# A hybrid decoder step on one core: new order of the recurrent block's activations, of the first norm's loads and of the sample rows

## What is computed

```
xn = rmsnorm(x, norm_mix)
lru_x, lru_g, q, k, v = split(xn @ w_in)
xc = causal_conv(x_ext, w_conv, b_conv)
r = sigmoid(block_diag(w_a) xc + b_a);  i = sigmoid(block_diag(w_x) xc + b_x)
log_a = -8 * r * softplus(-lam);  a = exp(log_a)
u = sqrt(-expm1(2 * log_a)) * i * xc        # factor 1 at position 0
h_t = a_t * h_(t-1) + u_t
y_lru = (h * gelu(lru_g)) @ w_branch_lru
```

## Time and profile before

| | |
|---|---|
| median of 3 runs | 1946.58 us (1945.2 to 1947.05) |
| the profiled execution | 1945.86 us, of which the span from first to last instruction is 1944.1 us |
| PE busy | 1918.2 us, 99% of the span |
| DVE, ACT, POOL busy | 1145.4, 616.8, 873.3 us |
| mean granted TensorE clock | 0.998 of full speed |
| chain that ended last | PE 88%, DVE 5% |

### The profile page before, as it was taken

One profiled execution on the slowest core, in us unless ns is written; L12 is line 12 of the kernel. 1 busy time (PEld: TensorE's weight loads), 2 busy tenths in 40 slices (PEclk: granted clock), 3 DMA queues, 4 the chain that ended last, 5 costly groups with the idle time before them and its releaser, 6 DMA issues.

```text
span 1944.1 us, 34565 instructions
## 1 busy us (share of the span) xinstructions
PE 1918.2 (99%) x13148; PEld 1870.2 (96%) x13148; DVE 1145.4 (59%) x1373; ACT 616.8 (32%) x1035; POOL 873.3 (45%) x533
## 2 busy tenths in 40 slices
PE   7999999999999999999999999999999999999999
PEld 7899999999999999999999999999999999999999
DVE  5666688878844545444328663586554555455555
ACT  5655632222203333333320111333222232223222
POOL 3233254444434433534334332336655656455643
PEclk9999999999999999999999999999999999999999
DMA  6111112222254355544345652112111111211112
GB/s 244 43 46 35 45 70 86 86 86 86 87 171 131 128 158 173 171 160 149 128 161 182 209 194 87 65 33 66 50 39 50 61 55 34 65 45 61 34 59 110
DMA packets 85034, 191.73 MB, mean 99 GB/s; under 512 B 10445, under 2 KB 38600, under 8 KB 83408
## 3 DMA queue, kind: packets, MB, share of 16 engines
q1 hardware_dynamic: 57872, 142.92, 22.3%
q10 hardware_dynamic: 27072, 47.53, 7.1%
HBM read 147.81 MB, written 42.62 MB: 98 GB/s over the span
## 4 chain that ended last, share of the span: by engine, by line
PE 88%; DVE 5%; issue 2%; DMA 1%; ACT 1%; POOL 1%; ACTq 1%; SPq 0%; DVEq 0%; POOLq 0%
PE ups L726 30%; PE ups L870 14%; PE ups L995 13%; PE ups L1038 11%; PE aux L1038 8%; PE aux L910 3%; PE ups L889 2%; PE aux L900 1%; PE ups L767 1%; PE aux L809 1%; DVE x L1583 1%; DMA big_f<-x_R 1%; PE aux L754 1%; PE ups L900 1%; ACTq L1090 1%
## 5 line engine op out<-in xcount | busy, mean ns | idle before, releaser
L726 PE MATMUL ups<-big,wsp 128*128 128x344 f32 x4680 | 755.1, 321 | 0.7 <-issue 0.7
L726 PEld LDWEIGHTS ups<-big,wsp 128*128 128x128 f32 x4680 | 739.9, 188 | 8.8 <-issue 1.6
L564 POOL CAST wsp<-wraw 128x1024 fp32r<-128x1024 f32 (+1 forms) x96 | 104.6, 1089 | 658.0 <-issue 393.9
L674 POOL TENSOR_TENSOR wsp<-wraw,wsp 128x512 fp32r<-128x512 f32 x184 | 263.7, 1449 | 212.4 <-ACT wsp L1406 212.4
L870 PE MATMUL ups<-big,wsp 128*128 128x344 f32 x1728 | 302.6, 326 | 0.0
L870 PEld LDWEIGHTS ups<-big,wsp 128*128 128x128 f32 x1728 | 271.4, 189 | 3.5 <-issue 3.0
L995 PE MATMUL ups<-big,wsp 128*128 128x344 f32 x1584 | 254.4, 320 | 0.3 <-DVEq L1979 0.2
L995 PEld LDWEIGHTS ups<-big,wsp 128*128 128x128 f32 x1584 | 248.9, 188 | 3.9 <-issue 2.9
L1038 PE MATMUL ups<-big,wsp 128*128 128x258 f32 x1920 | 240.7, 283 | 1.4 <-ACT ext L1445 1.3
L1038 PEld LDWEIGHTS ups<-big,wsp 128*128 128x128 f32 x1920 | 234.9, 189 | 1.8 <-issue 1.8
L566 POOL TENSOR_TENSOR wsp<-wraw,wsp 128x1024 fp32r<-128x1024 f32 (+1 forms) x96 | 228.7, 2382 | 7.7
(11 more groups left out here) (248 smaller groups left out, 1870.5 us busy)
## 6 DMA issues: line engine op xcount, KB each, us to landing
wraw<-w_in SPq DMA_DIRECT2D x52, 512.0 KB, 3.9
wraw<-w_ffn_in SPq DMA_DIRECT2D x80, 256.0 KB, 2.6
x<-out_qkv SPq DMA_DIRECT2D x35, 512.0 KB, 4.2
out_qkv<-x ACTq DMA_DIRECT2D x32, 512.0 KB, 3.3
wraw<-w_ffn_out SPq DMA_DIRECT2D x44, 256.0 KB, 2.8
x<-gate_s SPq DMA_DIRECT2D x16, 516.0 KB, 4.6
wraw<-w_merge SPq DMA_DIRECT2D x16, 512.0 KB, 6.7
x<-o_s SPq DMA_DIRECT2D x8, 792.0 KB, 4.8
```

The lines of the kernel that those rows point to most:

```text
L564: nc.gpsimd.tensor_copy(hi, raw).then_inc(w_hi, 1)
L674: nc.gpsimd.tensor_tensor(lo, raw_at(b), hi.bitcast(F32), ALU.subtract).then_inc(f_lo, 1)
L726: ins = nc.tensor.matmul(ups[:, slot, c, 0:CH], wsp[:, slot, w, k, :], src[:, a, k, c * CH:(c + 1) * CH], start=(k == 0 and n == 0), stop= ...
```

## The change

Four things are moved. In ACT's loop, gate chunk 0 of the next tile comes ahead of gelu and root, both of which now stand at the end of the iteration, and gates 1 and 2 follow each other; tanh is written to U instead of onto R. At the start, all x tiles are loaded ahead of weight tile (0,1), the rows of x ahead of weight tile (1,0); the lambda operations come first; DVE makes the low half of weight tile (0,0) and POOL's second split waits for six low halves of x; DVE squares row block 7, and a dummy root loads the table before block 6. The gate weights and the bias lines are issued by SP instead of ACT. The sample rows' work comes ahead of the last V tile, with its root one V tile earlier.

```diff
--- before.py
+++ after.py
@@ sync (SP's queue)
+            def gate_weights(i):
+                sp.wait_ge(gate_mm, i * NCH + 1)
+                for a, wn in enumerate(("w_rg_a", "w_rg_x")):
+                    src = A[wn][0].rearrange("n i j -> (n i) j")
+                    for h in range(2):
+                        sp.dma_start(bd[h * HD:(h + 1) * HD, a, h * HD:(h + 1) * HD],
+                                     src[ds(i * P + h * HD, HD), :]).then_inc(bd_loaded, 16)
-            sp.dma_start(gmix[:], A["c_norm_mix"]).then_inc(gm_ld, 16)
+            for dst, con in ((gmix[:], A["c_norm_mix"]), (par[:], A["c_par"])):
+                sp.dma_start(dst, con).then_inc(gm_ld, 16)
...
                 if name == "lru":
                     first = 2
                     weights(0, 0)
-                    x_tiles(0, 3)
+                    x_tiles(0, KT)
                     weights(0, 1)
-                    x_tiles(3, KT)
-                    for dst, con in ((par[:], A["c_par"]), (ident[:], A["c_ident"]), (x_rows[8], A["x_R"][SEQ:NT])):
+                    for dst, con in ((ident[:], A["c_ident"]), (x_rows[8], A["x_R"][SEQ:NT])):
                         sp.dma_start(dst, con).then_inc(par_ld, 16)
-                    weights(1, 0)
                     for n in range(4):
                         sp.dma_start(big2_f32[:, 0, 2 * n:2 * n + 2, 0:D],
                                      A["x_R"][2 * n * P:2 * (n + 1) * P].rearrange("(b p) d -> p b d", p=P)).then_inc(row_loaded[n], 16)
-                    weights(1, 1)
+                    weights(1, 0)
                     for dst, con in consts:
                         sp.dma_start(dst, con).then_inc(const_ld, 16)
+                    sp.wait_ge(bd_zero, 1)
+                    gate_weights(0)
...
+                    weights(1, 1)
...
+                if name == "qk":
+                    first = 1
+                    weights(0, 0)
+                    gate_weights(KT - 1)
+                    weights(0, 1)
                 with sp.Fori(first, iters) as i:
                     for slot in range(2):
                         weights(i, slot)
+                        if name == "lru" and slot == 0:
+                            gate_weights(i - 1)
@@ gpsimd
                 if name == "lru":
                     first = 1
-                    split(name, nk, 0, 0)
+                    pool.wait_ge(w_loaded[0], 16)
+                    nc.gpsimd.tensor_copy(wsp[:, 0, 0], wraw[:, 0]).then_inc(w_hi, 1)
+                    pool.wait_ge(xl_done, 6)
                     split(name, nk, 0, 1)
@@ scalar
...
+            act.wait_ge(gm_ld, 32)
             act.wait_ge(lam_dve, 1)
             nc.scalar.activation(lamt[:, 1, :], lamt[:, 0, :], ACT.Exp, scale=-1.0).then_inc(lam_act, 1)
             act.wait_ge(lam_dve, 2)
             nc.scalar.activation(lamt[:, 3, :], lamt[:, 2, :], ACT.Ln).then_inc(lam_act, 1)
...
             for k in range(KT):
                 high(k)
-            for b in range(SEQ // P + 1):
+            for b in (8, 0, 1, 2, 3, 4, 5):
                 square(b)
+            nc.scalar.activation(st[:, 0:1], epst[:], ACT.Sqrt)
+            square(6)
...
-            def side(i):
-                gate(i, 1)
+            def gelu(i):
                 act.wait_ge(ge_raw, i + 1)
                 nc.scalar.activation(GE, GE, ACT.Gelu_apprx_tanh)
-                gate(i, 2)
 
             def decay(i):
                 act.wait_ge(gate_ev, i * NCH + (NCH + 1))
                 apart(act)
-                step.step(nc.scalar.activation(AD, R, ACT.Exp, scale=cdec[:, 0, ds(i, 1)]))
-                apart(act)
-                nc.scalar.activation(R, R, ACT.Tanh, scale=cdec[:, 1, ds(i, 1)]).then_inc(ath_done, 1)
+                nc.scalar.activation(AD, R, ACT.Exp, scale=cdec[:, 0, ds(i, 1)])
+                nc.scalar.activation(U, R, ACT.Tanh, scale=cdec[:, 1, ds(i, 1)]).then_inc(ath_done, 1)
+                act.wait_ge(ath_done, i + 1)
+
+            def root_of(i):
                 act.wait_ge(m2_done, i + 1)
                 nc.scalar.activation(M2, M2, ACT.Sqrt).then_inc(sqrt_done, 1)
 
             with act.Fori(1, KT) as i:
-                step.loop(i, 1, 1)
-                side(i - 1)
-                gate_weights(i)
+                gate(i - 1, 1)
+                gate(i - 1, 2)
                 front(i)
                 decay(i - 1)
                 gate(i, 0)
-            step.end(KT - 1)
+                gelu(i - 1)
+                root_of(i - 1)
...
-            side(KT - 1)
...
+            gate(KT - 1, 1)
+            gelu(KT - 1)
+            gate(KT - 1, 2)
+            decay(KT - 1)
             first_evac()
-            act.wait_ge(m2_done, KT)
-            nc.scalar.activation(M2, M2, ACT.Sqrt).then_inc(sqrt_done, 1)
+            root_of(KT - 1)
...
                 if n == 2:
                     act.wait_ge(row_mm, 1)
                     nc.scalar.activation(QKR.rearrange("p a h e -> p (a h e)"), aux[0:RW, 1, 0:2 * P], ACT.Copy).then_inc(row_act, 1)
-                if n == 3:
                     act.wait_ge(row_dve, ROW_SQUARED)
@@ vector
-            for k in range(KT):
-                low(k)
-            dve.wait_ge(par_ld, 48)
-
+            dve.wait_ge(gm_ld, 32)
...
+            dve.wait_ge(w_hi, 1)
+            nc.vector.tensor_tensor(wsp[:, 0, 1], wraw[:, 0], wsp[:, 0, 0].bitcast(F32), ALU.subtract).then_inc(w_split[0], 1)
+            for k in range(KT):
+                low(k)
...
+            dve.wait_ge(row_loaded[3], 16)
+            step.step(nc.vector.tensor_tensor(x_rows[7], x_rows[7], x_rows[7], ALU.mult))
+            nc.vector.tensor_reduce(row_rms[:, 7:8], x_rows[7], AX_X, ALU.add).then_inc(nsq_done, 1)
             dve.wait_ge(nsq_done, SEQ // P + 2)
             nc.vector.reciprocal(row_rms, row_rms).then_inc(rr_done, 1)
...
-                nc.vector.scalar_tensor_tensor(M2, M2, 1.0, R, ALU.add, ALU.mult).then_inc(m2_done, 1)
+                nc.vector.scalar_tensor_tensor(M2, M2, 1.0, U, ALU.add, ALU.mult).then_inc(m2_done, 1)
...
-            v_in(3)
-            dve.wait_ge(ps_free[1], T0["att0"] + 1)
-            dve.wait_ge(u_sb, 2)
-            dve.sem_inc(pt_ev, 2)
...
+            dve.wait_ge(u_stored, 16)
+            dve.wait_ge(v_stored[1], 16)
+            dve.wait_ge(qn_stored[0], 16 * 13)
+            nc.vector.memset(VTOK[:, :, :, HD:HD + 1], 1.0)
+            v_in(3)
+            dve.wait_ge(ps_free[1], T0["att0"] + 1)
+            dve.wait_ge(u_sb, 2)
+            dve.sem_inc(pt_ev, 2)
+            for s, n in ((sa_done, 2), (pt_mm, 2), (pv_mm, 2), (o_ev, 1)):
+                dve.sem_inc(s, n)
```

More of the change, by code:

```diff
@@ L449, in _ @@
                                      A["x_R"][2 * n * P:2 * (n + 1) * P].rearrange("(b p) d -> p b d", p=P)).then_inc(row_loaded[n], 16)
-                    weights(1, 1)
+                    weights(1, 0)
                     for dst, con in consts:
                         sp.dma_start(dst, con).then_inc(const_ld, 16)
+                    sp.wait_ge(bd_zero, 1)
+                    gate_weights(0)
+                    sp.dma_start(lines.rearrange("p (g n) -> p g n", g=NG), A["c_lines"].rearrange("g b n -> b g n")).then_inc(lines_ld, 16)
+                    sp.dma_start(relx[0:NBK, :], A["rel_bias"]).then_inc(lines_ld, 16)
+                    sp.dma_start(relx[NBK:NBK + 1, :], A["c_one"]).then_inc(lines_ld, 16)
+                    weights(1, 1)
                 if name == "merge":
@@ L738, in norm_rows @@
                 pe.wait_ge(rr_done, 1)
-                pe.wait_ge(par_ld, 48)
+                pe.wait_ge(par_ld, 32)
                 for b in range(SEQ // P):
@@ L1084, in _ @@
             step = Chain(act, s_act)
[L1085 to L1091, removed]
             act.wait_ge(ones_done, 1)
             nc.scalar.activation(st[:, 0:1], epst[:], ACT.Copy)
-            act.wait_ge(gm_ld, 16)
+            act.wait_ge(gm_ld, 32)
+            act.wait_ge(lam_dve, 1)
+            nc.scalar.activation(lamt[:, 1, :], lamt[:, 0, :], ACT.Exp, scale=-1.0).then_inc(lam_act, 1)
+            act.wait_ge(lam_dve, 2)
+            nc.scalar.activation(lamt[:, 3, :], lamt[:, 2, :], ACT.Ln).then_inc(lam_act, 1)
             def high(k):
@@ L1105, in square @@
                 else:
-                    act.wait_ge(par_ld, 48)
+                    act.wait_ge(par_ld, 32)
                 n = x_rows[b].shape[0]
@@ L1189, in first_evac @@
                 nc.scalar.activation(sqkv[:, 0, :], tmp(0)[:, SEQ:NT], ACT.Copy).then_inc(sqc_done, 1)
-            side(KT - 1)
-            act.wait_ge(gate_ev, KT * NCH + 1)
-            step.step(nc.scalar.activation(AD, R, ACT.Exp, scale=cdec[:, 0, KT - 1:KT]))
-            nc.scalar.activation(R, R, ACT.Tanh, scale=cdec[:, 1, KT - 1:KT]).then_inc(ath_done, 1)
+            gate(KT - 1, 1)
+            gelu(KT - 1)
+            gate(KT - 1, 2)
+            decay(KT - 1)
             first_evac()
-            act.wait_ge(m2_done, KT)
```

(16 more changed lines are left out.)

## The result

The changed kernel takes 1952.49 us (median of 8 runs, 1951.06 to 1953.9), the kernel before beside it 1946.8 (8 runs, 1945.13 to 1947.3): 1.0032 times as long, 95% interval 1.0021 to 1.0043. The profiled spans are 1949.9 and 1944.1 us. The forecast was 1951.9.

A forecast was written before the change was run, and what follows sets the result against it. TensorE (PE) was taken as the bound, busy 1918.2 of 1944.1 us. Gains of 9.6 against losses of 14.9 gave +5.3 on the 1946.58 median: 1951.9 us, range 1944.0 to 1957.0 (the forecast case's own 1948.5 to 1955).

The forecast's parts named there:

- the gate waits: Recurrent loop: PE's waits of 1.33 and 1.15 us for gate(i,0)'s sigmoids vanish as the gate goes first, 2.5 us gained.
- slot at g + 16.25: Loop: PSUM slot 1 freed 16.25 us after PE's gates(i,0) start (g), needed at g + 14.6; 1.7 us wait each iteration.
- gate path: Loop: gate(i,1) stands behind the root, so PE's third gates wait 1.15 us, counted as lying inside the 1.7.
- Rival 1: Loop's slack holds, so only the gains stay: 1937.0 us, chance 0.12.
- rival 2: Start gives less, rows no earlier and clock still falls: gain 1.5 instead of 5.0, 1955.4 us, chance 0.14.
- rival 3: Loop: only the 1.15 of the gate path is paid because DVE's tail runs ahead: 1947.9 us, chance 0.05.
- rival 4: ACT's table switches each cost a drain as long as the load, 26.9 us more: 1978.8 us, chance 0.01.
- The hand-over: From recurrent loop to QK: the last root ends late, so PE waits 2.1 us for the statistics, 1.8 more than before.
- the loop's head: First iteration: a table load stands in front of a gate PE already awaits, 0.8 us lost (bounds 0 and 1.2).
- The norm: Start: x's rows land sooner and the row norm comes at 32.7, gain 3.4 us (bounds 2.2 and 4.9).
- The clock after the norm: Start: a stand cut to 1.5 us no longer drops PE's clock to half, 1.6 us saved (bounds 0 and 1.6).
- The sample rows: Before the first scores: the row work moves into DVE's idle time ahead of the last V tile, 2.1 us gained.

The follow-up runs named there:

- a_old_order: Changed kernel with ACT's loop back in the old order (gelu, then root ahead of gate 0), all else as changed: 1939.98 us, ratio 0.9965.
- b_loop_alone: Kernel before with only ACT's new loop order and tanh to U, gate weights still issued by ACT: 1959.31 us, ratio 1.0066.
- r2_root_ahead: Changed kernel with root ahead of gelu behind gate 0, run once more for its trace: 1946.92 us.
- q_peeled: Changed kernel with gelu ahead of gate 0, first and last turn written out of the loop, last turn's root ahead of its gate 0: 1936.28 us, ratio 0.9948.
- w_warm: Changed kernel with 24 dummy 128 x 128 matmuls on PE ahead of the first tile: 1953.23 us, ratio 1.0037.
- v_gelu_ahead: Changed kernel with gelu moved ahead of gate 0 in ACT's loop, root still behind that gate: 1939.57 us, ratio 0.9961.
- s_start_alone: Changed kernel with ACT's old loop order and the sample rows back behind the last V tile: 1945.4 us, ratio 0.9991.
- r_root_ahead: Changed kernel with root ahead of gelu behind gate 0, the product waiting for gelu: 1945.93 us, ratio 0.9993.

## Why the prediction was right, point by point

**Right in its sum and in the loop.** For the order in ACT's queue the prediction had 14.9 us of losses and 2.5 of gain at the gate waits, 12.4 net. Between the two traces, from gates(0,0) to the second statistics, it is 12.0 (230.0 after, 218.1 before); the medians of a_old_order and b_loop_alone give 12.5 and 12.4, with what the clock takes behind the stands in them. The turn was put at 27.8 us and is 27.87; root at g + 8.5 (g + 8.53), slot at g + 16.25 (g + 16.25), gate path 1.15 (1.13). The terms were durations in series on ACT and then on DVE, each with an uncontended row, and that is why they held. Two smaller sizes were off and offset each other only in part. The first turn costs less, 27.32 (66.29 to 93.61), as PE waits for the slot six times and not seven. The two gate waits bring more than their 2.5: the turns with them take 27.74 and 27.55 instead of 26.13, 3.0 together. Rival 1 (the slack holds) needed this chain to be shorter; rival 2 (a norm after 34 with a fallen clock) didn't happen, the norm is at 33.18; rival 3 is what r2_root_ahead does, which takes gelu out of the root's path; rival 4 (a drain at each table switch) has no time to stand in, as the loads and activations of the rows above follow one another without a gap.

**The hand-over** was put at 2.1 us of wait and is 2.41; **the loop's head** at 0.8 and is 0.64. q_peeled takes both away.

**The norm**: 2.9 instead of 3.4. The last chunk of rows came at 30.03 rather than 29.5. A wrong step stood beside it: "PE done with tile 7 some 2 us earlier", from which followed that PE was ready at 31.2. PE was ready at 32.87. The change feeds x faster, but some thirty matmuls at the start are slow whatever feeds them (w_warm). The upper bound of 4.9 for this gain was therefore out of reach. More than that, "worth nothing while the rows arrive last" holds only in some executions. With the same loads, the last chunk was there at 28.9 to 29.2 us in v_gelu_ahead, q_peeled, r2_root_ahead and s_start_alone, and PE came to the norm without a wait at 32.42 to 32.89 (also in a_old_order, at 33.12):

```profile
32.42 1.95 PE L763 MATMUL aux<-ident,big_f 128*128 128x128 f32 x16
```

There PE's own work is what the norm waits for, and earlier rows would bring nothing.

**The clock after the norm**: 1.6 predicted. From row norm to gates(0,0) it is 13.96 us before (36.09 to 50.05) and 12.73 after (33.18 to 45.91), so 1.2. And it is no fixed property of the kernel before: b_loop_alone has the same start, stood for 2.77 us at the same place, and the clock (the column behind PE's) stayed:

```profile
36.13 2.05 PE L741 MATMUL aux<-ident,big_f 128*128 128x128 f32 x16 [2.77 <-DVE big_f L1544]
...
37.00:38.00 1.00, 1.00 (x11) 1.00 0.00 0
```

Its 16 matmuls take 2.05 us, where the earlier trace rows has 3.17. This term should have had a chance beside its price.

**The sample rows** are the term that was mis-sized: 2.1 predicted, 3.7 between the two traces. The wait was counted and the clock behind it was not, though the prediction had done so for the norm. (1.33 leaves the clock alone, 2.94 doesn't) gave no side for 2.11; the windows behind the wait would have. But the 1.6 is not a certain part either: in b_loop_alone PE stood 2.10 us at the same place and the clock stayed at 1.00. By the same rule the hand-over's new wait of 2.41 has a price beyond its length in some executions: behind 2.40 in b_loop_alone the clock fell, behind 2.41 in the changed kernel's profiled execution it did not. The prediction left this out too, with the opposite sign.

**What made up for it.** The running difference was +4.1 at 592.86 us, 1.1 under the forecast's, and +5.8 at the end. The 1.7 between them lie in the feed-forward loop, which the change doesn't touch (the chain that ended last, start and length):

```profile
1417.27 17.22 PE ups L995 x108
...
1606.57 17.22 PE ups L995 x108
```

```profile
1421.38 17.22 PE ups L1017 x108
...
1611.55 17.22 PE ups L1017 x108
```

Three turns take 189.30 us before and 190.17 after, 63.10 or 63.39 each. Over nine turns the kernel before took 569.6 us, the changed one 571.3, and the experiments from 570.0 to 572.3. What makes a turn 0.28 longer wasn't found; no idle time of PE is shown there. So the profiled total agrees with the forecast better than its terms do, and that part is luck. Against the forecast the start gave 0.9 us less and the turns 2 to 7 cost 0.9 less, the hand-over cost 0.4 more; the sample rows gave 1.6 more, and the feed-forward loop, which is in no term, took 1.7.

## What to carry to other kernels

When an instruction that waits for the bound engine moves ahead in a queue, add up everything that is queued behind it up to what frees that engine's next buffer; the slack has to hold all of it. A cheap order puts ahead of the waiting gate whatever is ready (gelu here), and only then what must be behind it. In this case a stand of TensorE of two to three microseconds is priced as its length plus a chance of some 1.5 us more, lost to half clock behind it.

## What the runs showed of the hardware

**Slow first matmuls under a clock column of 1.00.** In the changed kernel the first matmuls of 344 columns take 519 ns in the mean (9.5 to 11 us), later ones 318 (17 to 19 us):

```profile
L789 PE MATMUL ups<-big,wsp 128*128 128x344 f32 x5 | 1.8, 519 | 9.5 <-DVE big L1533 9.5
...
L789 PE MATMUL ups<-big,wsp 128*128 128x344 f32 x15 | 2.5, 318 | 0.0
```

The windows of 9 to 11 us give the clock as 1.00 all the same. Matmuls issued before them take the slowness away (w_warm: 330 ns in the mean from 9.5 to 11). The Trainium skill, page "TensorE: Matmul & The Clock Gate", Part 1, has an idle TensorE at 1.2 GHz; the durations fit that (four of the same size took 488 ns in v_gelu_ahead from 264 to 266 us, under a clock of 0.50), the clock column doesn't.

**Behind a stand of two to three microseconds the clock fell in some executions and not in others.** All stands of PE over 1 us between 20 and 620 us in ten traces (all but that of r_root_ahead), with the granted clock of the windows behind them:

| stand, us | the clock fell to 0.50 behind it | it stayed at 1.00 |
|---|---|---|
| 1.07 to 1.63 | none | 6 |
| 2.10 to 2.94 | 7 (2.11, 2.12, 2.36, 2.36, 2.40, 2.45, 2.94) | 4 (2.10, 2.41, 2.43, 2.77) |

The same stand falls on either side: 2.40 and 2.45 at the second statistics lost the clock, 2.41 and 2.43 at the same place did not. Each fall left two or three whole windows of 1 us at 0.50, with a partly lowered one beside them, and cost 1.2 to 1.6 us: from the row norm to gates(0,0) it is 13.96 us with a fall and 12.73 to 12.75 without, from the first scores to the second transposes 5.78 to 5.80 and 4.27 to 4.28. The mean clock of the other runs tells the same without a trace: in q_peeled and r_root_ahead, whose kernels show no stand over 1.07 us, it is 1.000 in each of the runs behind their medians; in the changed kernel, with its one stand of 2.41, it is 0.999 in six of eight (1951.99 to 1953.9 us) and 1.000 in two (1951.06 and 1951.69, the profiled one). What decides it within this range was not found.

**POOL and DVE run longer side by side.** L1614, 128 x 8 elements, takes 0.17 us in the loop and 2.18 under POOL's L586; POOL's own operation is longer too, 4.25 us where it takes 2.4 alone. The Trainium skill, page "SBUF — State Buffer", section "Who interferes with whom", calls the ports that both share an exclusive lock: it names operations with two inputs, and copies that can run in a two-port mode, as those that contend. The trace agrees: a COPY of 128 x 6 was held as well (2.31 us at 33.18, under POOL's 2.37 from 33.09).
